# Queries stored in token and in class order, mask tables built during the projection, the first head's loads spread, and the sums of gates moved behind the first pass

## What is computed

```python
h = rmsnorm(x, norm_g)
proj = jnp.einsum('bld,de->ble', h, w_in)      # q, k, v, z of the delta group; q, k, v, z of the window group
# group A: short conv + silu, l2-normalised q and k, gated delta rule in chunks
decay = jnp.exp(jnp.where(incl, gc[..., :, None] - gc[..., None, :], -jnp.inf))
attn = jnp.einsum('bhnid,bhnjd->bhnij', q, k) * decay
o_a = rmsnorm(o_a, dn_norm_g) * jax.nn.silu(z_a)
# group B: 8 heads of 64, three windows: every key back 128, every 4th back 512, every 16th back 2048
parts = [dilated_branch_prompt(qb, kb, vb, w // d, d) for w, d in ((128, 1), (512, 4), (2048, 16))]
o_b = merge_dilations(parts) * jax.nn.silu(z_b)
y = rmsnorm(x + jnp.einsum('ble,ed->bld', concat(o_a, o_b), w_out), final_norm_g)
```

## Time and profile before

| | us |
|---|---|
| median of 3 runs | 1940.05 |
| the three runs | 1942.07, 1934.40, 1940.05 |
| profiled execution, whole | 1935.3 |
| its span | 1933.6 |
| PE busy in the span | 1739.5 (90%) |
| DVE, ACT, POOL busy | 835.5, 640.2, 371.9 |
| granted TensorE clock, mean | 0.933 |

### The profile page before, as it was taken

The page is one execution under the profiler, slowest core; times in us unless marked ns, Lnnn a source line. Parts: engine busy times, 40 slices in busy tenths (PEclk is TensorE's granted clock), DMA queues, the critical chain, the costliest instruction groups (busy, mean ns, idle before and its releaser), DMA issues. The chain is left out here.

```text
span 1933.6 us, 27678 instructions
## 1 busy us (share of the span) xinstructions
PE 1739.5 (90%) x9686; PEld 1432.3 (74%) x9686; DVE 835.5 (43%) x1904; ACT 640.2 (33%) x1550; POOL 371.9 (19%) x388
## 2 busy tenths in 40 slices
PE   5999999999999999968788899889899568889897
PEld 5998878888888888846678778778877446667674
DVE  3535312521441253139853453444443464445452
ACT  4524222411331142111424344444345223333332
POOL 0000000000000000037142341341342342432331
PEclk9999999999999999988798898999899568999998
DMA  5425686787468868777856636645430476665660
GB/s 170 131 61 134 139 267 191 144 205 218 109 174 228 212 145 184 216 230 237 235 135 163 163 86 146 170 113 113 120 110 17 142 212 178 192 163 174 163 201 27
DMA packets 227546, 310.10 MB, mean 160 GB/s; under 512 B 62892, under 2 KB 176044, under 8 KB 217948
## 3 DMA queue, kind: packets, MB, share of 16 engines
q1 hardware_dynamic: 222820, 300.15, 58.4%
q10 hardware_dynamic: 4608, 8.39, 1.2%
HBM read 228.50 MB, written 146.97 MB: 194 GB/s over the span
## 5 line engine op out<-in xcount | busy, mean ns | idle before, releaser
L342 PE MATMUL pj<-hT_hi,w_hi 128*128 128x512 f32 x896 | 361.8, 404 | 1.8 <-DVE raw L595 1.8
L343 PE MATMUL pj<-hT_lo,w_hi 128*128 128x512 f32 x896 | 354.6, 396 | 0.0
L344 PE MATMUL pj<-hT_hi,w_lo 128*128 128x512 f32 x896 | 354.3, 395 | 0.0
L344 PEld LDWEIGHTS pj<-hT_hi,w_lo 128*128 128x128 f32 x896 | 168.4, 188 | 40.8
L342 PEld LDWEIGHTS pj<-hT_hi,w_hi 128*128 128x128 f32 x896 | 168.6, 188 | 39.6 <-issue 2.1
L343 PEld LDWEIGHTS pj<-hT_lo,w_hi 128*128 128x128 f32 x896 | 168.8, 188 | 36.8
L1161 POOL TENSOR_TENSOR gm<-upto,g_hi 128x512 fp32r<-128x512 f32 x16 | 16.6, 1040 | 840.3 <-POOLq L2590 839.9
L1412 PE MATMUL o_ps<-pt,vt 128*65 128x256 f32 (+3 forms) x560 | 149.3, 393 | 3.2 <-DVE ot L1679 2.2
L1514 ACT ACTIVATE pt<-pt_ps 128x512 f32<-128x512 f32 x144 | 84.7, 588 | 162.4 <-PE pt_ps L1390 161.9
L2316 PE MATMUL y_bank<-wo_hi,mh 128*128 128x512 f32 (+1 forms) x272 | 113.1, 416 | 6.8 <-POOL ml L2301 4.6
L557 DVE SCALAR_TENSOR_TENSOR acc<-raw,conv_wt,acc 128x512 f32<-128x512 f32 x144 | 108.3, 752 | 5.1
(11 more groups left out here) (460 smaller groups left out, 3585.1 us busy)
## 6 DMA issues: line engine op xcount, KB each, us to landing
out_dram<-in_cache_k_win_dram SPq DMA_DIRECT2D x56, 584.0 KB, 8.2
out_dram<-in_cache_v_win_dram SPq DMA_DIRECT2D x56, 584.0 KB, 8.8
w_raw<-in_w_in_dram SPq DMA_DIRECT2D x31, 512.0 KB, 12.3
kq_all<-sil SPq DMA_DIRECT2D x32, 256.0 KB, 5.2
wqk<-hi SPq DMA_DIRECT2D x32, 256.0 KB, 5.3
wqk<-lo SPq DMA_DIRECT2D x32, 256.0 KB, 5.1
sc_class<-kq_all SPq DMA_DIRECT2D x16, 512.0 KB, 5.1
qs<-wqk SPq DMA_DIRECT2D x16, 512.0 KB, 7.9
```

The costliest lines, as they stand in the source:

```text
L342: pe.matmul(out, w_hi[s][:, k, :], hT_hi[:, k, cols], start=(k == 0), stop=False)
L343: pe.matmul(out, w_hi[s][:, k, :], hT_lo[:, k, cols], start=False, stop=False)
L344: mm = pe.matmul(out, w_lo[s][:, k, :], hT_hi[:, k, cols], start=False, stop=(k == KT - 1))
```

## The change

- Queries are stored a second time in class order. In a wq tile ACT copies the high part from `hi` into `sil` in class order, and DVE the low part from `lo` into `acc`; SP stores both to a new tensor `wq_class`. The two buffers `qs` of whole heads become one `q_tok` (token order, near units) and one `q_class` (class order, far units), and the far units read contiguous weights.
- The near and class tables are made in `g_row` during tiles 6, 13 and 20 of the projection (POOL: four iotas; DVE: 9 + 9 + 6 instructions), stored at tile 21, and loaded as one tensor at the start of the mixers. DVE's tables in the first pass are gone.
- Of head 0, kh and kl are loaded piece by piece behind the ring loads of chunks 0 to 3, `q_tok` at chunk 4, `q_class` at chunk 8. Later heads load `q_class` at the start of the head before, and `q_tok` two heads ahead once the near units that read it are masked. `g_dn` is loaded behind `zb`.
- The sums of gates, with `sample_gates` and the six exponents, stand behind the last score of head 0 (PSUM `d_ps`), and POOL's masks and memsets behind its last chunk.

```diff
@@ project, scalar, wq tile
+                        if kind == "wq":
+                            act.wait_ge(hi_done, 8 * j + c + 1)
+                            act.wait_ge(post_done, posts_before(j, "v", c) + 1)
+                            act.wait_ge(sil_stored[c], 16 * (3 * j + 2))
+                            act.activation(by_class(sil[:, c, :]), from_tokens(hi[:, c % 2, :].bitcast(F32)), ACT.Copy).then_inc(class_hi_done, 1)
@@ project, vector
+                if t in TABLES_AT[0:2]:
+                    class_half(TABLES_AT.index(t))
+                elif t in TABLES_AT:
+                    near_half()
...
+                        if kind == "wq":
+                            dve.wait_ge(pj_free[c], t + 1)
+                            dve.wait_ge(sil_done, 4 * (3 * j + 3))
+                            at_least(dve, class_lo_stored[c % 2], 16 * (2 * j + c // 2))
+                            dve.tensor_copy(by_class(acc[:, c % 2, :]), from_tokens(l.bitcast(F32))).then_inc(class_lo_done, 1)
@@ loads of a head
-QK_DMAS, V_DMAS, KQ_DMAS, CHUNK_DMAS = 6, 4, 1, 5
+K_DMAS, Q_DMAS, V_DMAS, KQ_DMAS, CHUNK_DMAS = 4, 2, 4, 1, 5
...
+def load_q_class_from(sp, D, env, h):
+
+    for part in range(2):
+        sp.dma_start(env.operands[1][HD * part:HD * part + HD, :].bitcast(F32), D.wq_class[part, bass.ds(HD * h, HD), :]).then_inc(env.q_class_in, 16)
@@ mixers, sync
-            load_qk_from(sp, D, E, 0, 0)
-            with nc.allow_non_contiguous_dma(reason="one column"):
-                sp.dma_start(E.g_dn[:], D.dn_norm_g.unsqueeze(1)).then_inc(g_dn_in, 16)
+            sp.dma_start(E.tables[:], D.tables).then_inc(tables_in, 16)
             for c in range(NT):
+                if c == 8:
+                    load_q_class_from(sp, D, E, 0)
...
+                if c < 4:
+                    load_k_piece_from(sp, D, E, 0, 0, c)
+                if c == 4:
+                    load_q_tok_from(sp, D, E, 0)
...
-            load_qk_from(sp, D, E, 1, 1)
+            load_k_from(sp, D, E, 1, 1)
+            sp.wait_ge(S["masked"], S_CREDIT + 8)
+            load_q_tok_from(sp, D, E, 1)
...
             load_z_from(sp, D, E, 0)
+            with nc.allow_non_contiguous_dma(reason="one column"):
+                sp.dma_start(E.g_dn[:], D.dn_norm_g.unsqueeze(1)).then_inc(g_dn_in, 16)
...
                 h = 2 * i + e
-                if more:
+                ahead = more or e == 0
+                if ahead:
                     sp.wait_ge(S["masked"], S_CREDIT + UNITS * (h + 1))
                     sp.sem_inc(S["seen"], 1)
-                    load_qk_from(sp, D, env, h + 2, e)
+                    load_q_class_from(sp, D, env, h + 1)
+                if more:
+                    load_k_from(sp, D, env, h + 2, e)
@@ score, far units
-                        pe.matmul(out[:, at:at + w], in_tokens(qs[e][:])[:, r, b], by_step(kh[e][:])[:, r, 0:b + 1], start=True, stop=False)
+                        pe.matmul(out[:, at:at + w], by_step(q_class[:])[:, r, b], by_step(kh[e][:])[:, r, 0:b + 1], start=True, stop=False)
@@ mixers, tensor
-                if c == 5:
-                    sums_of_gates()
-                if c == min(EARLY):
-                    pe.wait_ge(sums_exped, 6)
...
+                elif step == "spread":
+                    sums_of_gates()
@@ mixers, vector
-                if c == 2:
-                    near_table()
-                if c == 3:
-                    class_steps()
-                if c == 4:
-                    sample_gates()
-                    class_table()
...
             gather_corners(NT - 1)
-            dve.wait_ge(masks_made, 2)
-            dve.wait_ge(g_dn_in, 16)
             for step, *a in FIRST_SCORES:
                 if step == "score":
                     score(0, a[0])
+                    if a[0] == 14:
+                        sample_gates()
...
+            negative_decay()
+            dve.wait_ge(masks_made, 2)
+            dve.wait_ge(g_dn_in, 16)
             walk(dve, attend, delta)
```

More of the change, by code:

```diff
@@ L245, in _ @@
             for t, j, y, kind in TILES:
+                if t == TABLES_AT[2] + 1:
+                    sp.wait_ge(table_done, 3)
+                    sp.dma_start(D.tables, g_row[:, 0:2 * P + CHUNK]).then_inc(tables_out, 16)
                 if t + 2 < NTILES:
@@ L298, in _ @@
                 pool.affine_select(out=t[:], in_=t[:], compare_op=op, fill=0.0, base=0, pattern=[[step, P]], channel_multiplier=-step).then_inc(tables, 1)
+            pool.wait_ge(gate_step, GATE_STEPS)
+            for x in range(2):
+                if x:
+                    pool.wait_ge(table_done, x)
+                pool.iota(near_tab.bitcast(I32), pattern=[[-1, 2 * P]], base=CHUNK - P - 2 * P * x, channel_multiplier=1).then_inc(iota_done, 1)
+            pool.wait_ge(table_done, 2)
+            pool.iota(row_at, pattern=[[0, 1]], base=0, channel_multiplier=1).then_inc(iota_done, 1)
+            pool.iota(near_tab.bitcast(I32), pattern=[[P, 2], [1, CLASSES], [CLASSES, RUN]], base=-P, channel_multiplier=0).then_inc(iota_done, 1)
         @block.tensor
@@ L829, in mixer_operands @@
     H = DN_HEADS
-    qs = [sb(f"qs{e}", [P, SEQ], F32R) for e in range(2)]
+    q_tok, q_class = sb("q_tok", [P, SEQ], F32R), sb("q_class", [P, SEQ], F32R)
     kh = [sb(f"kh{e}", [P, SEQ], F32R) for e in range(2)]
@@ L888, in load_tokens_from @@
 def load_tokens_from(sp, D, env, c, e):
[L890 removed]
+    ktok, vtok, za = env.operands[7:]
     t = bass.ds(P * c, P)
@@ L903, in mixers @@
         E, H, ident = env, DN_HEADS, env.ident
-        qs, kh, kl, vt, zb, kq, ktok, vtok, za = env.operands
+        q_tok, q_class, kh, kl, vt, zb, kq, ktok, vtok, za = env.operands
         qk_in, ring_in, near_v_in, class_v_in, z_in, chunk_in = env.qk_in, env.ring_in, env.near_v_in, env.class_v_in, env.z_in, env.chunk_in
@@ L1032, in head @@
                     load_near_v_from(sp, D, env, h + 1)
+                if more:
+                    sp.wait_ge(S["masked"], S_CREDIT + UNITS * (h + 1) + 8)
+                    sp.sem_inc(S["seen"], 1)
+                    load_q_tok_from(sp, D, env, h + 2)
                 for u in range(2):
@@ L1337, in score @@
                 if k == 0:
-                    pe.wait_ge(qk_in[e], 16 * QK_DMAS * loads)
+                    pe.wait_ge(qk_in[e], 16 * K_DMAS * loads)
+                    pe.wait_ge(E.q_tok_in, 16 * Q_DMAS * (h + 1))
                     pe.wait_ge(S["maxed"], h + 1)
+                if k == 8:
+                    pe.wait_ge(E.q_class_in, 16 * Q_DMAS * (h + 1))
                 pe.wait_ge(S["masked"], UNITS * h + k + 1)
@@ L2608, in hybrid_step @@
     D.k_tok, D.v_tok = scratch("k_tok", [SEQ, QK_W]), scratch("v_tok", [SEQ, QK_W])
+    D.wq_class = scratch("wq_class", [2, SW_WIDTH, SEQ])
+    D.tables = scratch("tables", [P, 2 * P + CHUNK])
     D.wqk, D.mix = scratch("wqk", [2, 2, SW_WIDTH, SEQ]), scratch("mix", [D_MODEL, SEQ])
```

155 lines of the change are left out of this document (90 added, 65 removed).

## The result

The changed kernel takes 1944.59 us (median of 20 runs), the kernel before 1939.75 us (20 runs beside them): ratio 1.0030, 95% interval 1.0018 to 1.0042. The profiled execution has a span of 1939.8 us against 1933.6, 6.2 more.

| stretch | before | after | difference |
|---|---|---|---|
| start of the span to DVE's first cast of the mixers (T0) | 842.58 | 841.39 | -1.2 |
| T0 to the load of the corners (first pass) | 85.1 | 82.3 | -2.8 |
| load of the corners to the substitution | 12.2 | 30.2 | +18.0 |
| substitution to the products of the state in chunk 0 | 54.3 | 63.1 | +8.8 |
| these to the same products in chunk 15 (walk) | 486.3 | 472.4 | -13.9 |

The account below looks back on a forecast made before the run. It took DVE and transfers in turns to bound the first pass and first scores, and PE the walk. The profiled 1935.3 + 14.6 - 14.7 gave 1935.2; the median was put at 1939, range 1918 to 1953.

Parts of the forecast that it names:

- First pass, 15 us: First pass of the mixers: 15 us gained (10 to 21), as chunk 2's store wait and the table work go.
- The term of chunk 8: First pass: chunk 8 starts at 879 to 881 in place of 898.86, a gain of 18 to 20 us.
- The sum by transfers: First pass: q_tok's landing from transfers queued ahead, 873 if stores cost nothing, 882 with seven chunks' stores.
- third rival: First pass stays bound by stores landing behind key pieces; its gain shrinks by 11 to 13, median 1951; chance 0.14.
- The term of `q_class`: First pass from chunk 8: q_class puts 5.2 us of transfers between ring loads, 4 counted as lost.
- g_dn: Before the substitution: DVE idles some 19 us for the column, landing 31.7 us behind the corners' load; start 4.5 us later.
- q_class of head 1: Before head 1's first far unit: PE stands 8.1 us for this load, plus 2 us at half clock.
- Far scores, 14.7: Far units in the walk: contiguous weights load faster, 2.1 us a head, 14.7 us gained over seven heads (8 to 19).
- first rival: Before the substitution: g_dn's stall misses PE or the column lands early; first pass's 15 us stay, median 1920; chance 0.18.
- the second: Rival at head 1's far units: q_class is there in time, up to 8 us less, 1931; chance 0.12.
- the fourth: Rival at the far scores: weights load as slowly from q_class, 14.7 us are missing, 1954; chance 0.06.
- the two that it named as making the forecast wrong: Substitution (L1668) starting before 930, or the walk from 1024 to 1500 not getting shorter by 8 us or more.

Follow-up runs that it names:

- the one with two queues: Kernel with g_dn and head 1's q_class early, second chunk behind the inverse, head 0 in one go; three upper-half loads moved to ACT's queue: 1918.90 us, ratio 0.9891.

## Why the prediction was wrong

- **Projection, 0**: held. T0 is 1.2 us earlier, inside its scatter, and PE's waits there are 1.8 us (2.7 before).
- **First pass, 15 us**: this step failed; 2.8 came. The term of chunk 8 was the wrong one. From T0 it starts at 48.2 us, before at 56.3: 8.1 gained, not 18 to 20. The tables (11.79) and chunk 2's wait (9.63) did go, 21.4 in all; but waits of 3.05, 1.25, 2.67, 2.94 and 4.15 us, 14.1 in all, came into chunks 2 to 6. The sum by transfers went by one deadline, `q_tok`, and put it at 873 to 882; that was right, PE's first product with it ran at 881.20. But chunk 7 was taken to be waiting there, and DVE was only in chunk 6 (881.51), because each chunk had a deadline of its own, the landing of the stores behind whatever narrow piece was ahead. That is the third rival's mechanism, at the landings it named (attn 9.5 and 8.2 us in the windows 840 to 864 and 864 to 885), and its price of 11 to 13 us is what was missing. The term of `q_class` was about right: 4 expected, and from chunk 8 to chunk 15 28.9 us against 23.6, 5.2 lost.
- **g_dn**: the mechanism and the size held. 31.7 us from the corners' load were expected, 30.2 measured; DVE idle 19, measured 18.26. It started 9.4 us later than forecast only because the corners' load was issued at 923.64, 11.0 us later than forecast, and 1.5 us came back in this stretch. (The terms given for the 31.7 us add up to 31.5.) By the runs it costs 17 us in the kernel after and 23 (16 to 30) alone.
- **q_class of head 1**: 8.1 and 2 us expected, 6.91 us of wait and 8.8 in the stretch measured.
- **Far scores, 14.7**: 13.9 in the two traces, 15 by the run with the stride restored, with the width given there.
- **The sum**: 14.6 - 14.7 became 24.0 - 13.9, and with the two outer stretches (-1.2, -2.8) the 6.2 us between the spans. The 12.2 us missing from the first pass alone would have given the third rival's 1951; that it came out at 1944.6, so near the forecast, is in part luck, since the other misses (-1.2, -1.5, -1.3, +0.8, -2.8) nearly all go the other way and come to 6 us. The 1 us by which the forecast lay under the old median is not in its sum, which gives 0.1. The first rival fell with the column's landing of 20.7 us and PE's wait of 18.79, the second with 6.91 us, the fourth with the run that restored the stride. Of the signs that the prediction named, those of the first pass failed: chunk 8 was to be near 880 and came at 889.61, the last chunk near 907 and came at 918.46. Neither of the two that it named as making the forecast wrong would have caught a first pass that is too long.

What would have told it ahead stands in the prediction's own numbers: in chunks 0 to 4 a narrow piece or more (2.6 us each), a ring load (1.1) and the stores (1.3) make 5.0 us of transfers a chunk, and DVE paces at 3.1 to 3.4. Chunks 2 to 6 went by at (881.51 - 859.60) / 4 = 5.5 us.

## What to carry to other kernels

Ask of every transfer that is moved what it stands behind and which wait it ends; its size says nothing, and a load that is wanted late can still be the one that everything waits for. When a stall is ended by a landing in a queue that is full, moving the loads that fill it spreads the stall; only fewer or faster bytes shorten it. Where two stalls lie behind one another in such a queue, their removal is costed together, since an earlier transfer takes its place from a third.

## What the runs showed of the hardware

- Transfers that fill 64 partitions moved at about 215 GB/s, with the DMA engines busy for over 0.98 of the time; transfers of 128 partitions of the same size moved at 400. Stores from the other queue waited with them: those of `attn` landed after 9.5 us between 840 and 864, and after 3.9 in the kernel before between 885 and 905, where no narrow load was in flight.
- A transfer whose outermost dimension is two moved at some 52 GB/s.
- A weight load of 128 x 128 fp32 in the scores takes 188 ns from neighbours and 320 to 329 ns from every fourth element.
- The walk, with the same work for PE in all of them, comes in two lengths: 472 to 473 us in nine of eleven profiles with contiguous far weights, 478 in the other two. The first 144 us tell them apart by the granted clock, here for the kernel with the second chunk behind the inverse and for the one with two queues (length, busy PE, PEld, DVE, ACT, POOL, clock, DMA share, GB/s):

```profile
994.50:1066.50 72.00, 63.02 (x451) 56.44 (x452) 34.71 (x117) 29.52 (x83) 26.03 (x31) 0.93 0.68 165
1066.50:1138.50 72.00, 65.24 (x455) 56.76 (x454) 34.19 (x111) 33.94 (x85) 22.63 (x26) 0.93 0.60 147
```

```profile
993.30:1065.30 72.00, 63.03 (x438) 57.00 (x439) 32.65 (x108) 29.00 (x82) 23.99 (x29) 0.88 0.71 165
1065.30:1137.30 72.00, 65.78 (x439) 57.59 (x438) 33.18 (x114) 30.84 (x78) 22.37 (x26) 0.88 0.59 148
```

  0.93 against 0.88: in these 144 us PE got through 906 matmuls of the same stream in the one and 877 in the other. What decides which of the two comes was not found, and 5 us of a difference between single profiles can be this alone.
- Not settled: whether transfers that fill different halves of the partitions at one time would run at full rate together; and how much of the stores' shorter waits with loads of 128 partitions comes from reading no key row twice.
